# Byte offsets of the operands of a two-block transformer kernel: every Strassen product reads its moving operand at 64 and its weights at 128 modulo 256

## The reference, cut to what matters

```python
def swiglu(x, w_gate, w_up, w_down):
    return (jax.nn.silu(x @ w_gate) * (x @ w_up)) @ w_down

def swiglu_ffn(h, w_gate_up, w_down):
    g, u = jnp.split(h @ w_gate_up, 2, axis=-1)
    return (jax.nn.silu(g) * u) @ w_down

for i in range(DEPTH):                      # first block: two FFNs a layer
    h = rmsnorm(x, g_ffn1_pre[i])
    x = x + 0.5 * rmsnorm(swiglu(h, w1_gate[i], w1_up[i], w1_down[i]), g_ffn1_post[i])
    ...
    h = rmsnorm(x, g_ffn2_pre[i])
    x = x + 0.5 * rmsnorm(swiglu(h, w2_gate[i], w2_up[i], w2_down[i]), g_ffn2_post[i])
...
for i in range(DEPTH):                      # second block: one FFN a layer
    x = hybrid_layer(x, mem, positions, i, *layers[i])
```

## Time and profile before

| | us |
|---|---|
| median of 3 runs | 3319.55 (3316.45 to 3319.96) |
| the profiled execution | 3313.52 |
| its span, first to last instruction | 3312.4 |
| PE busy in it | 3199.0 (97%) |
| DVE, ACT, POOL busy | 2052.8, 1359.3, 1349.4 |

### The profile page before, as it was taken

The page is one execution under the profiler, slowest core; times in us unless marked ns, Lnnn a source line. Parts: engine busy times, 40 slices in busy tenths (PEclk is TensorE's granted clock), DMA queues, the critical chain, the costliest instruction groups (busy, mean ns, idle before and its releaser), DMA issues.

```text
span 3312.4 us, 50521 instructions
## 1 busy us (share of the span) xinstructions
PE 3199.0 (97%) x19480; PEld 2724.8 (82%) x19487; DVE 2052.8 (62%) x2671; ACT 1359.3 (41%) x2335; POOL 1349.4 (41%) x643
## 2 busy tenths in 40 slices
PE   8999999999999999999999999998999999999998
PEld 6998875789977899877579987765689987879987
DVE  6774444577646876355477765678477733477753
ACT  5553225344435455322434543324434531154542
POOL 6320562544116541065174404656554107735300
PEclk9999999999999999999999999999999999999999
DMA  4543221145332454322025533211145433215532
GB/s 156 157 148 106 89 88 33 64 152 158 116 124 83 129 169 122 105 83 89 14 102 153 157 115 113 102 64 39 45 140 155 135 106 110 83 46 153 163 117 96
DMA packets 99965, 362.50 MB, mean 109 GB/s; under 512 B 11088, under 2 KB 11344, under 8 KB 99536
## 3 DMA queue, kind: packets, MB, share of 16 engines
q1 hardware_dynamic: 88704, 320.90, 29.0%
q0 software_dynamic: 7776, 28.32, 5.1%
q10 hardware_dynamic: 3312, 10.86, 0.9%
HBM read 355.84 MB, written 4.19 MB: 109 GB/s over the span
## 4 chain that ended last, share of the span: by engine, by line
PE 76%; DVE 9%; POOL 4%; ACT 4%; issue 4%; DMA 3%; DVEq 0%; ACTq 0%; POOLq 0%; SPq 0%
PE psC L754 4%; PE psC L756 4%; PE psC L755 4%; PE psA L754 4%; PE psA L756 4%; PE psA L755 4%; PE psD L904 2%; PE psD L906 2%; PE psD L905 2%; PE psB L904 2%; PE psB L906 2%; PE psB L905 2%; PE psC L904 2%; PE psC L906 2%; PE psC L905 2%
## 5 line engine op out<-in xcount | busy, mean ns | idle before, releaser
L634 POOL TENSOR_TENSOR WH<-raw,scalars 128x1024 fp32r<-128x1024 f32 (+1 forms) x194 | 379.1, 1954 | 1192.3 <-DMA raw<-in_w 1127.0
L2247 DVE TENSOR_TENSOR WL<-raw,WH 128x1024 fp32r<-128x1024 f32 x324 | 441.4, 1365 | 74.6 <-POOL raw L668 46.4
L636 POOL TENSOR_TENSOR WL<-raw,WH 128x1024 fp32r<-128x1024 f32 (+1 forms) x194 | 472.4, 2435 | 15.2
L1702 ACT ACTIVATE WH<-raw 128x1024 fp32r<-128x1024 f32 x324 | 340.7, 1054 | 37.4 <-DMA raw<-in_ws 25.8
L2323 DVE TENSOR_TENSOR WL<-raw,WH 128x1024 fp32r<-128x1024 f32 (+1 forms) x144 | 163.1, 1135 | 291.9 <-ACT WH L1723 291.5
L663 POOL TENSOR_TENSOR raw<-raw,Y 128x1024 f32<-128x1024 f32 x54 | 133.7, 2476 | 509.1 <-DMA raw<-in_ws 509.1
L1723 ACT ACTIVATE WH<-raw 128x1024 fp32r<-128x1024 f32 (+1 forms) x144 | 141.8, 988 | 346.4 <-DMA raw<-in_w 346.4
L754 PE MATMUL psA<-HH,WH 128*128 128x512 f32 x560 | 229.9, 410 | 0.0
L756 PE MATMUL psA<-HL,WH 128*128 128x512 f32 x560 | 218.4, 390 | 0.0
L755 PE MATMUL psA<-HH,WL 128*128 128x512 f32 x560 | 218.0, 389 | 0.0
L904 PE MATMUL psD<-TH,WH 128*128 128x256 f32 x720 | 200.6, 279 | 2.3 <-ACT psD L1742 2.0
(11 more groups left out here) (536 smaller groups left out, 9622.1 us busy)
## 6 DMA issues: line engine op xcount, KB each, us to landing
raw<-in_w SPq DMA_DIRECT2D x338, 512.0 KB, 3.5
raw<-in_ws SPq DMA_DIRECT2D x216, 512.0 KB, 3.6
Y<-in_ws SPq DMA_DIRECT2D x54, 512.0 KB, 4.6
raw<-in_ws POOLq DMA_DIRECT2D x54, 512.0 KB, 5.4
X<-in_x ACTq DMA_DIRECT2D x4, 512.0 KB, 9.9
NRAW<-in_mem ACTq DMA_DIRECT2D x2, 1024.0 KB, 6.8
out<-Y SPq DMA_DIRECT2D x8, 256.0 KB, 2.1
POSI<-in_pos ACTq DMA_DIRECT2D x4, 256.0 KB, 2.6
```

The costliest lines, as they stand in the source:

```text
L634: pool.tensor_tensor(WH[j][:, 0:w], raw[j][:, 0:w], zero[:, 0:1].broadcast_to([P, w]), ALU.subtract).then_inc(w_hi, 1)
L636: pool.tensor_tensor(WL[j][:, 0:w], raw[j][:, 0:w], WH[j][:, 0:w], ALU.subtract).then_inc(w_split, 1)
L1702: act.activation(WH[slots[i]][:], DX if i == 6 else raw[slots[i]][:], ACT.Copy).then_inc(part_hi, 1)
L2247: dve.tensor_tensor(WL[slots[i]][:], DX if i == 6 else raw[slots[i]][:], WH[slots[i]][:], ALU.subtract).then_inc(part_lo, 1)
```

## The change

HH and HL move by 64 bytes with `top8` put ahead of them; each ring slot is followed by a gap of 64 bytes, and three of the four gaps hold 48 columns each of what was `VALL` (VEC0 to VEC2, the rest is VEC3). The slots 11 to 14 are new views that begin 64 bytes into ring slots 0 to 3. The products take their weights from those views and from slots 8, 9 and 10. So every product has (64, 128), and plain and down pieces have (64, 64).

```diff
     X = sb("X", [P, KD, S])
+    top8 = sb("top8", [P, QB, 8])
+    region(LINE // 2)
     HHo, HLo = region(16 * KB), region(16 * KB)
...
-    slot_at = [region(8 * KB) for _ in range(RING)]
+    slot_at, vecs = [], []
+    for j in range(RING):
+        slot_at.append(region(8 * KB))
+        region(LINE // 2)
+        if j < RING - 1:
+            vecs.append(sb(f"VEC{j}", [P, NVEC]))
...
-    VALL = sb("VALL", [P, DEPTH * NV + NW])
+    identb = sb("identb", [P, P], BF16)
+    vecs.append(sb("VEC3", [P, DEPTH * NV + NW - 3 * NVEC]))
...
+    slot_at += [o + LINE // 2 for o in slot_at[0:RING]]
...
-    sum_at = [ar + 48 * KB - 9 * LINE // 2, ar + 56 * KB - 9 * LINE // 2, ar + 72 * KB - LINE // 2, ar + 80 * KB - LINE // 2]
+    sum_at = [ar + 48 * KB - 2 * LINE, ar + 56 * KB - 2 * LINE, ar + 72 * KB, ar + 80 * KB]
...
-    PART_SLOTS = (8, 0, 1, 9, 2, 10, 3)
-    LAST_PLAIN_OF_RING = lambda normed: 7 if normed else 4
+    part_slots = lambda normed: (12, 13, 14, 11, 8, 9, 10) if normed else (13, 14, 11, 12, 8, 9, 10)
...
                 load(SPARE + 1, RING + 2)
-                load(RING - 1, 3)
+                load(0, RING + 2)
                 load(SPARE, 3)
-                used = (2, 3, 5)
+                used = (2, 3, 5, 7)
             else:
                 ring(RING + 2)
                 load(SPARE, RING)
                 load(SPARE + 1, RING)
-                used = (3, 5, 5)
+                used = (3, 4, 5, 6)
...
             part(a2, v, 0, a2_in)
+            sp.wait_ge(piece_used, plain + used[3])
             part(b, v, 3, b_in)
...
-            for j, products in enumerate((2, 1, 2, 2)):
-                sp.wait_ge(part_used, n.full(part_used, products))
-                sp.nop(nofuse=True)
+            sp.wait_ge(part_used, n.full(part_used, 4))
+            for j in range(RING):
                 load(j, RING, down_in)
...
-        load(VALL[:], A["vec"], vec_in)
+        for i in reversed(range(len(vecs))):
+            load(vecs[i][:], A["vec"][:, i * NVEC:DEPTH * NV + NW if i == 3 else (i + 1) * NVEC], vec_in)
...
             def pair(p, first=False, last=False):
...
-                if first:
-                    act.wait_ge(piece_used, n.now(piece_used) + LAST_PLAIN_OF_RING(normed))
-                    act.nop(nofuse=True)
-                else:
+                if not first:
                     quad_gate(3, pair_banks(p + 1)[2])
```

More of the change, by code:

```diff
@@ L147, in sb @@
         return nc.alloc_sbuf_tensor_at(name, list(shape), dt, offset=o)
-    KB, LINE = 1024, 128
+    KB, LINE, NVEC = 1024, 128, 48
     X = sb("X", [P, KD, S])
+    top8 = sb("top8", [P, QB, 8])
+    region(LINE // 2)
     HHo, HLo = region(16 * KB), region(16 * KB)
@@ L158, in program @@
     YSS = sb("YSS", [P, S])
-    identb = sb("identb", [P, P], BF16)
-    region(LINE // 2)
     SQo = region(4 * KB)
@@ L176, in program @@
     stat = sb("stat", [P, 8, 4])
-    top8 = sb("top8", [P, QB, 8])
     WIT = sb("WIT", [P, QB, IDXH], offset=RYo)
-    region(5 * LINE // 2)
     ar = region(88 * KB)
-    slot_at += [ar + 72 * KB, ar + 80 * KB, ar + 28 * KB, ar + 36 * KB, ar + 64 * KB - 7 * LINE // 2, SQo, Yo + 8 * KB]
+    slot_at += [ar + 72 * KB, ar + 80 * KB, ar + 28 * KB, ar + 36 * KB, ar + 64 * KB - 3 * LINE // 2, SQo, Yo + 8 * KB]
+    slot_at += [o + LINE // 2 for o in slot_at[0:RING]]
     alike = lambda x, y, ahead=0: (y - x - ahead) % (2 * LINE) == 0
     assert all(alike(slot_at[j], o) for j in range(RING + 4) for o in (HHo, HLo, ar))
-    assert all((slot_at[j] - HHo) % (4 * LINE) == 5 * LINE // 2 for j in (8, 9, 10))
+    assert all(alike(slot_at[0], slot_at[j], LINE // 2) for j in range(RING + 4, len(slot_at)))
     raw = [sb(f"raw{j}", [P, TILES * P], offset=o) for j, o in enumerate(slot_at)]
@@ L191, in program @@
     BF = sb("BF", [P, KD, S], offset=ar + 8 * KB)
-    sum_at = [ar + 48 * KB - 9 * LINE // 2, ar + 56 * KB - 9 * LINE // 2, ar + 72 * KB - LINE // 2, ar + 80 * KB - LINE // 2]
-    assert all(alike(o, slot_at[0], LINE // 2) for o in sum_at)
+    sum_at = [ar + 48 * KB - 2 * LINE, ar + 56 * KB - 2 * LINE, ar + 72 * KB, ar + 80 * KB]
     TF = [sb(f"TF{i}", [P, HALF_K, HALF], offset=o) for i, o in enumerate(sum_at)]
@@ L310, in program @@
     W_AT = DEPTH * NV
-    w_col = lambda c: VALL[:, W_AT + c:W_AT + c + 1]
+    vec_at = lambda c, i: c - i * NVEC
+    columns = lambda c, w=1: vecs[min(c // NVEC, 3)][:, vec_at(c, min(c // NVEC, 3)):vec_at(c, min(c // NVEC, 3)) + w]
+    w_col = lambda c: columns(W_AT + c)
     at_layer = [0]
-    v_col = lambda c: VALL[:, at_layer[0] * NV + c:at_layer[0] * NV + c + 1]
+    v_col = lambda c: columns(at_layer[0] * NV + c)
     C_CONV, C_SQ, C_SK, C_SV, C_CQ, C_KR = 0, 8, 10, 12, 14, 19
@@ L555, in ffn @@
             nonlocal turn
-            slots = PART_SLOTS
+            slots = part_slots(normed)
             if normed:
@@ L594, in ffn @@
             n.full(part_lo, PRODUCTS)
+            sp.wait_ge(part_used, n.full(part_used, 4))
             turn = 0
-            for j, products in enumerate((2, 1, 2, 2)):
-                sp.wait_ge(part_used, n.full(part_used, products))
-                sp.nop(nofuse=True)
+            for j in range(RING):
                 load(j, RING, down_in)
+            n.full(part_used, 3)
             with n.loop(DOWN_PIECES // RING - 1):
@@ L688, in ffn @@
                 split(SPARE + 1, TILES)
-                split(RING - 1, TILES)
+                split(0, TILES)
                 split(SPARE, TILES)
@@ L697, in ffn @@
                 split(SPARE + 1, TILES)
-                pool.wait_ge(piece_used, n.full(piece_used, 6))
-                n.full(piece_used, FFN_PIECES - 6)
+                pool.wait_ge(piece_used, n.full(piece_used, 5))
+                n.full(piece_used, FFN_PIECES - 5)
             sums(slots, True)
@@ L947, in ffn @@
                 pe.wait_ge(gu_free, n.room(gu_free))
-                whole(gate_bank(3), RING - 1)
+                whole(gate_bank(3), 0)
                 whole(up_bank(3), SPARE)
@@ L1970, in attend @@
             n.full(pv_done, len(pairs))
-        act.wait_ge(vec_in, 16)
+        act.wait_ge(vec_in, 64)
         act.wait_ge(consts_ok, 1)
@@ L2677, in _ @@
         dve.memset(epsc[:], EPS).then_inc(consts_ok, 1)
-        dve.wait_ge(vec_in, 16)
+        dve.wait_ge(vec_in, 64)
         for k in range(KD):
@@ L2693, in _ @@
         for layer in range(DEPTH):
-            post = VALL[:, layer * NV:layer * NV + 2 * KD]
+            post = columns(layer * NV, 2 * KD)
             step(dve.tensor_scalar(post, post, 0.5, None, ALU.mult))
```

## The result

The changed kernel takes 3324.36 us (median of 20 runs, 3317.64 to 3329.74), the one before 3317.65 us (20 runs, 3308.81 to 3329.14): ratio 1.0018, 95% interval 1.0009 to 1.0026. It is slower by 6.7 us by the medians. Faster by 6.8 had been forecast.

What follows compares the result with a forecast made beforehand. PE, busy 97% of the span, was taken as the bound; -8.0 + 0 + 0 + 1.2 + 0 = -6.8 us on 3319.55 gave 3312.75, say 3312.5 us, range 3304.5 to 3326.5.

Steps and rivals of the forecast that it cites:

- The state is kept where no border flips it: PE's products: without HH/TH address borders a stretch keeps its last wait's spacing; pairs 0.38 us shorter or 0.39 longer.
- So these pairs can keep the gain: Free pairs: P2's slack behind the seeded copy falls from 0.64 to 0.26 us, since loads move up with PE.
- I take the 21 pairs as short: Free pairs of FFNs 0, 4 and 5: the second pair's wait leaves the short spacing; 21 x -0.38 = -8.0 us.
- the long state is locked in: Rival, slower: stretches entering long stay long until their next wait; all 33 free pairs long gives +14.1, 3333.6 us; chance 0.15.
- the pairs outside the 21: 12 free pairs in FFNs 1 to 3 taken as even, 0, bounds 4.6 us either way; the rest wait.
- The cover of the gain: Shorter products count only where nothing else ends last on PE: 33 of 54 pairs were taken as free.
- the others wait: Pairs outside the 33 wait for loads, sums, splits and the seeded copy; shorter products there only lengthen a wait.
- The start: ACT issues four transfers ahead of X instead of one: three more issues, uncovered, 3 x 0.41 = +1.2 us.
- The bound of 1.7: Upper bound for the kernel's start: three more issues at the price of an issue of X, 3 x 0.56.
- Columns of 512, slots, down loads: 512-column matmuls 0, bound 3.9 us both ways; slots and waits 0, up to +2.0 if late; down loads 0.

Runs made afterwards that it cites:

- More slack alone: ACT's splits for P6 and P3 put ahead of the gate: on the kernel before 3302.69 us (ratio 0.9948), on the changed kernel 3310.57 us (0.9972).
- the first two experiments: Kernel before with gains in four DMAs: 3321.38 us, ratio 1.0005; changed kernel with only the first norm's gains ahead of X: 3320.00 us.
- the second profile with both edits: Changed kernel with only first-norm gains ahead of X and ACT's splits for P6 and P3 ahead of the gate: 3309.28 us; second profile's run 3309.07.

## Why the prediction was wrong

*The state is kept where no border flips it: right.* All seven products of a pair run alike (pairs of 19.04 and of 19.79), and HH no longer differs from TH. That a border in the weights' offset resets it, in most cases, is shown by putting one back at P0 (14 of 19, against 1 of 203 without it).

*"So these pairs can keep the gain": the step that failed.* It took a slack of 0.26 us as lasting, since a pair's loads are issued from the ends of PE's products. In FFNs 0, 4 and 5 the wait of P2 in the second pair did leave the short spacing, as forecast; but in the trace after, the slack falls from 0.68 to 0.13 within one short pair, P2 is held up, and the short spacing is gone by the seventh, the fourth and the fourth pair. The term of -8.0 us for these 21 pairs measures +7.0 in the two profiled executions. One of the loads isn't tied to PE's products: `d` goes into a buffer that DVE has to read first (its split for P6). Timelines of SP's issues, `a`, `d` and `c` of a short pair, of one that lost its slack, and of a long one; behind them POOL's first sum, which needs `c` and `d`:

```profile
109.61 0.33 SPq L557 DMA_DIRECT2D raw<-in_ws  x1
111.28 0.33 SPq L557 DMA_DIRECT2D Y<-in_ws  x1
112.30 0.33 SPq L557 DMA_DIRECT2D raw<-in_ws  x1
...
147.88 0.33 SPq L557 DMA_DIRECT2D raw<-in_ws  x1
150.60 0.33 SPq L557 DMA_DIRECT2D Y<-in_ws  x1
151.19 0.33 SPq L557 DMA_DIRECT2D raw<-in_ws  x1
...
1178.33 0.33 SPq L557 DMA_DIRECT2D raw<-in_ws  x1
1179.77 0.33 SPq L557 DMA_DIRECT2D Y<-in_ws  x1
1181.13 0.33 SPq L557 DMA_DIRECT2D raw<-in_ws  x1
```

```profile
117.57 2.40 POOL L669 TENSOR_TENSOR raw<-raw,Y 128x1024 f32<-128x1024 f32 x1 [10.31 <-DMA raw<-in_ws]
...
158.14 2.39 POOL L669 TENSOR_TENSOR raw<-raw,Y 128x1024 f32<-128x1024 f32 x1 [11.55 <-DMA raw<-in_ws]
...
1185.99 2.39 POOL L669 TENSOR_TENSOR raw<-raw,Y 128x1024 f32<-128x1024 f32 x1 [10.21 <-DMA raw<-in_ws]
```

From `c`'s issue to the sum it is 5.27, 6.95 and 4.86 us. As the splits slip behind PE, `d` is issued later, close to `c`, and both land later: the chain lengthens just when PE is ahead of it. That `d` next to `c` is what makes them slow was only read from these rows, not tried.

*"I take the 21 pairs as short": it failed with that.* A wait draws again, and a late step of less than 0.1 us is enough. In FFN 5's fourth pair the second matmul of P2 starts 0.18 us after the first, in place of 0.11, and the products are long from there on (timeline of PE):

```profile
3071.49 0.34 PE L910 MATMUL psB<-TH,WH 128*128 128x256 f32 x1
3071.67 0.28 PE L911 MATMUL psB<-TH,WL 128*128 128x256 f32 x1
```

Not each one does it: at 131.07, as late, the pair stayed short. Long pairs leave 1.01 us of slack, so nothing draws again behind them, and short pairs run on until they wait. So in this execution each FFN ends long, whatever it began with: five of the six were long from somewhere between the second and the fifth pair on, the other from the seventh. The rival "the long state is locked in" came true in its main part; that short stretches don't last was not in it. Its price was 14.1 us with the start. The pairs and the start measure 7.1 + 3.4 = 10.5: some pairs were still short, and in FFNs 1 to 3 pairs that had waited before ran long without waiting. That the pairs outside the 21 changed by only 0.1 us together, near the forecast 0, is a balance of gains and losses, and luck. Of FFN 3 the prediction counted the wait in the second pair; the last wait before its free pairs, in the fourth, had left the long spacing, but no term rested on that.

*The cover of the gain.* More slack alone took 10 us off the pairs of the kernel before, nearly all of it in FFNs 1 to 3, and the waits on the copy off PE's list in the changed kernel: the chain to P2, and not PE's spacing, set the pairs of FFNs 1 to 3. That had been counted as "the others wait", with no price.

*The start: right in its place, mis-sized.* 3 x 0.41 = 1.2 was the delay of the issue (1.66 measured); the landing moved by 3.44. The bound of 1.7 took X's flight as fixed, but it grew from 6.9 to 8.7 us. SP issues six weight loads in the same first 4.5 us, and X, issued later, has more of them ahead of it. That reading is argued, and the small packets of the four transfers (768 under 512 B at the start, 208 before) may have a share; that the three issues make the start late, by 3.4 us and more, is shown by the first two experiments.

*Columns of 512, slots, down loads: as forecast, 0.* Outside the pairs and the start the profiled execution after takes 5.2 us less than the one before. Most of it, 3.8 us, lies between the first down matmul of FFN 2 and the first product of FFN 3 (446.5 us, 450.3 before), where the mean granted clock was 0.99 of full speed after and 0.98 before: of its two levels, 2.4 and 1.2 GHz, the lower one holds for 7 us there after and for 17 before. Such stretches differ by as much between executions of one program here, so it isn't put down to the change.

In the two profiled executions the pairs cost 7.1 us and the start 3.4, less the 5.2 elsewhere: 5.4 in all. By the medians the change costs 6.7 us, of which 4.4 go with X put ahead; the parts are near what these runs can tell, so only the traces divide them.

## What to carry to other kernels

When a stage becomes faster, follow every load of the next round back to what releases it: a slack that holds at the old pace can shrink in each round until it is gone. A quick pace that has nothing to bring it back is lost sooner or later to a disturbance, while a slower pace that causes no waits is kept; a cheap, regular reset can be worth more than removing what looks like a penalty, if the chain behind has slack for it. And DMA issues put ahead of a transfer at the kernel's start can cost more than their own issue time: three of them, 1.7 us of issuing, made it land 3.4 us later here.

## What the runs showed of the hardware that was not expected

Matmuls of one shape at one pair of offsets (64, 128) have two steady spacings, 113 and 118 ns, that last through more than a thousand matmuls (FFN 5 of the second profile with both edits: seven pairs at 19.04). One program with this choice in each of six FFNs, worth 5.7 us an FFN (179.2 against 173.5), took 3296 to 3320 us from run to run; part of that spread lies outside the pairs. A matmul that starts 0.07 us late can turn the short spacing into the long one. With the weights of one product in seven 64 bytes off the others (and two slots exchanged for it), the next product was short again in every pair, once the FFN's first pairs were over, and the time went from 3309 to 3292 us. The Trainium skill says in "TensorE: Matmul & The Clock Gate", section "Step-by-step: what each phase is for", that loading the next weights takes no read bandwidth from the running matmul. No run here measures that bandwidth, but the rule alone doesn't account for the spacing: with nothing moved but P0's weights, from 192 to 0 modulo 256, P0 went from 2.84 us to 2.72 in most pairs.
